# The end of a recurrence rebuilt: head outputs split first, fetches in order of need, spatial weights in their own buffers

## The reference, cut to what matters

```python
a = _rms_norm(h, g_mix[l])
p = a @ w_in[l]
p_sgu, p_rwkv, p_gate = jnp.split(p, [2 * D_A, 2 * D_A + C_B], axis=-1)
y_a = _sgu_branch(p_sgu, ...)      # z = gelu(p_sgu); u, v = split(z); v = layer_norm(v) * w + b
                                   # per chunk of 128 tokens and group of 128 columns:
                                   # s = u * (tril(sgu_w) @ v + sgu_b);  y_a = s @ w_proj_a
y_b = _rwkv7_branch(p_rwkv, ...)   # a recurrence over tokens, 16 heads of 64;  y_b = o @ w_proj_b
mixed = sigmoid(gate_a) * y_a + sigmoid(gate_b) * y_b
h = h + mixed @ w_out[l]           # then a feed-forward net and the last norm
```

## Time and profile before

| | |
|---|---|
| median of 3 runs | 3925.5 us (3919.31 to 3929.22) |
| profiled execution | 3924.53 us; its span 3922.7 us, so 1.8 us lie around the span |
| PE busy | 3692.0 us, 94% of the span |
| DVE, ACT, POOL busy | 1805.7, 1325.9, 295.7 us |
| mean granted clock of PE | 0.976 of full speed |
| chain that ended last | PE 86%, DVE 5%, ACT 5%, issue 2%, DMA 1% |

### The profile page before, as it was taken

The page is one execution under the profiler, slowest core; times in us unless marked ns, Lnnn a source line. Parts: engine busy times, 40 slices in busy tenths (PEclk is TensorE's granted clock), DMA queues, the critical chain, the costliest instruction groups (busy, mean ns, idle before and its releaser), DMA issues.

```text
span 3922.7 us, 53647 instructions
## 1 busy us (share of the span) xinstructions
PE 3692.0 (94%) x23179; PEld 3000.0 (76%) x23179; DVE 1805.7 (46%) x2513; ACT 1325.9 (34%) x2053; POOL 295.7 (8%) x328
## 2 busy tenths in 40 slices
PE   7989999988899998999998999998999999599998
PEld 6777888867678886888886778886877777478887
DVE  4334434444443444543343344344656656445443
ACT  4444322333332232232234443224332333343222
POOL 1001100100010011110010011012000000000001
PEclk9999999989999999999999999998999999799999
DMA  6212323311122332332331123233222212332332
GB/s 208 65 49 70 97 91 102 96 55 52 61 92 91 100 100 75 97 94 90 103 96 54 52 78 97 92 97 98 78 58 62 79 53 67 125 111 89 104 94 69
DMA packets 333231, 337.44 MB, mean 86 GB/s; under 512 B 11857, under 2 KB 323779, under 8 KB 332484
## 3 DMA queue, kind: packets, MB, share of 16 engines
q1 hardware_dynamic: 332578, 333.89, 27.6%
q10 hardware_dynamic: 418, 0.12, 0.0%
HBM read 319.29 MB, written 14.68 MB: 85 GB/s over the span
## 4 chain that ended last, share of the span: by engine, by line
PE 86%; DVE 5%; ACT 5%; issue 2%; DMA 1%; ACTq 0%; POOL 0%; SPq 0%; POOLq 0%; DVEq 0%
PE P L99 85%; ACT sA L114 2%; ACT hi L113 1%; PE P L102 1%; DVE lo L117 1%; DVE x L117 0%; DVE mp L122 0%; DVE ds L125 0%; DVE rw_S L117 0%; DMA scr<-held_dram 0%; ACTq L154 0%; ACT scr L114 0%; DMA vg<-held_v_dram 0%; DVE st L134 0%; DMA rows<-in_shift_b_dram 0%
## 5 line engine op out<-in xcount | busy, mean ns | idle before, releaser
L117 DVE TENSOR_TENSOR lo<-raw,hi 128x1024 fp32r<-128x1024 f32 (+2 forms) x617 | 738.7, 1198 | 1177.6 <-ACT hi L113 1176.9
L99 PE MATMUL P<-aH,lo 128*128 128x512 f32 x2840 | 1142.6, 402 | 28.6 <-DVE q L125 11.4
L99 PE MATMUL P<-aH,hi 128*128 128x512 f32 x2840 | 1114.6, 392 | 0.0
L99 PE MATMUL P<-aL,hi 128*128 128x512 f32 x2840 | 1114.4, 392 | 0.0
L113 ACT ACTIVATE hi<-raw 128x1024 fp32r<-128x1024 f32 (+2 forms) x617 | 610.5, 991 | 1033.3 <-PE P L99 1027.2
L99 PEld LDWEIGHTS P<-aH,lo 128*128 128x128 f32 x2840 | 538.7, 190 | 160.8 <-issue 21.2
L99 PEld LDWEIGHTS P<-aH,hi 128*128 128x128 f32 x2840 | 538.0, 189 | 115.3
L99 PEld LDWEIGHTS P<-aL,hi 128*128 128x128 f32 x2840 | 539.3, 190 | 111.6 <-issue 5.4
L99 PE MATMUL P<-bH,lo 128*128 128x512 f32 x1088 | 426.1, 392 | 16.0 <-DVE bL L117 16.0
L99 PE MATMUL P<-bH,hi 128*128 128x512 f32 x1088 | 424.9, 391 | 0.0
L99 PE MATMUL P<-bL,hi 128*128 128x512 f32 x1088 | 424.9, 391 | 0.0
(11 more groups left out here) (284 smaller groups left out, 3884.5 us busy)
## 6 DMA issues: line engine op xcount, KB each, us to landing
raw<-in_w_ffn_in_dram SPq DMA_DIRECT2D x176, 512.0 KB, 3.5
raw<-in_w_in_dram SPq DMA_DIRECT2D x163, 512.0 KB, 3.8
raw<-in_w_ffn_out_dram SPq DMA_DIRECT2D x96, 384.0 KB, 3.0
raw<-in_w_ffn_dram SPq DMA_DIRECT2D x36, 512.0 KB, 3.6
raw<-in_w_o_dram SPq DMA_DIRECT2D x26, 512.0 KB, 3.5
raw<-in_w_ffn_dram SPq DMA_DIRECT2D x32, 384.0 KB, 3.1
raw<-in_w_mem_kv_dram SPq DMA_DIRECT2D x16, 512.0 KB, 4.3
raw<-in_w_ffn_out_dram SPq DMA_DIRECT2D x16, 512.0 KB, 3.4
```

Of the source, the lines that this page charges most:

```text
L99: return self.e.matmul(out, l, r, start=start, stop=stop, skip_group_check=skip) if self.e else Nothing()
L117: return self.e.tensor_tensor(out, a, b, op) if self.e else Nothing()
```

## The change

- `rw_store` of all eight pairs stands ahead of everything else behind the recurrence. On ACT the eight `bH` splits now come before the gelu of v.
- The last 12 triples of the held products are told to need the end of pair 6, so they go behind the recurrence and no longer between its last steps.
- SP's fetches have a new order: v in four pieces, each with its own semaphore; the spatial weights, the two norm vectors and the bias; the first two tiles of u; the first four gates; then `x`, which came first.
- `wsn` no longer lies in a buffer of the recurrence, nor does `hold1`; `wsn` has a semaphore of its own.
- The layer norm took three DVE operations of 1024 columns a tile (subtract and scale, times weight, plus bias). It now takes two of each half (`scalar_tensor_tensor` of 128x512), first all first halves, then all second halves; groups 0 to 3 of `sgu_mix` need only the first. The inverse deviation is made by one Ln and one Exp over all four tiles.
- The planner's numbers for `side` changed, and with them where its steps fall among the triples.

The diff, cut to its core:

```diff
-    side = [Step("load_v", needs=[("end", 6)], lat=1.0)]
-    side += [Step("rw_store", p, lat=0.8, needs=[("end", p)], gives=[("o", 6)] if p == 6 else []) for p in range(7)]
-    side += [Step("sgu_stats", q, lat=3.0) for q in range(4)]
-    side += [Step("rw_store", 7, lat=0.8, needs=[("end", 7)], gives=[("o", 7)]), Step("sgu_load")]
-    side += [Step("load_gate", i) for i in range(4)] + [Step("load_u", g, needs=[("held",)]) for g in range(2)]
-    side += [Step("sgu_turn", pe=0.9, lat=2.0)] + [Step("sgu_norm", q, lat=2.5) for q in range(4)]
+    side = [Step("load_v", needs=[("end", 6)])]
+    side += [Step("rw_store", p, far=0.0, dve=0.62, wait=0.7, hold=p == 7, needs=[("end", p)], gives=[("o", p)]) for p in range(8)]
+    side += [Step("sgu_load"), Step("first_u", needs=[("held",)]), Step("load_gates"), Step("load_x_back")]
+    side += [Step("sgu_gelu", q, lat=3.0 if q == 0 else 1.0) for q in range(4)] + [Step("first_gates")]
+    side += [Step("sgu_stats", q, dve=1.5, hold=True) for q in range(4)] + [Step("sgu_inverse", lat=7.0), Step("sgu_turn", pe=0.9, dve=1.4, hold=True)]
+    side += [Step("sgu_norm", q, 0, dve=1.55, hold=True) for q in range(4)]
+    side += [Step("sgu_norm", q, 1, far=0.0, dve=1.55, gives=[("ln", q)]) for q in range(4)]
     for g in range(8):
-        side += [Step("sgu_mix", g, pe=1.8, lat=1.0, far=3.5, gives=[("sgu", g)])]
+        side += [Step("sgu_mix", g, pe=1.8, needs=[("ln", 3)] if g >= 4 else [], lat=1.0, far=3.5, dve=1.3, gives=[("sgu", g)])]
...
+    held = jobs_steps(held_jobs(), 1)
+    for s in held[len(held) - 12:]:
+        s.needs += (("end", 6),)
...
-        e.dma(m["vg"][:, :, :], d["held_v"]).then_inc(*S.v_in.up(0, by=16))
+        for q in range(4):
+            e.dma(m["vg"][:, q, :], d["held_v"][:, q, :]).then_inc(*S.v_in[q].up(0, by=16))
...
+        e.stt(y, y, ag[:, 0:1], m["lnw"][:, n], ALU.subtract, ALU.mult).then_inc(*S.evict.up())
+        e.wait_ge(*S.act_turn.at("ln"))
         e.wait_ge(*S.evict.now())
+        e.stt(y, y, rs, m["lnb"][:, n], ALU.mult, ALU.add).then_inc(*S.evict.up(("ln", q, j)))
...
-    at("wsn", [8, 128], off=big + 16384 + 12288)
-    at("wsT", [8, 128], off=ex)
+    at("wsn", [8, 128], off=ex)
+    at("wsT", [8, 128], off=ex + 4096)
...
-    at("hold1", [S_], off=regions[-1][0])
+    at("hold1", [S_], off=ex + 8192)
```

More of the change, by code:

```diff
@@ L450, in the_order @@
     pairs = [[s for p in range(u, 8, 2) for s in pair_steps(p, u)] for u in range(2)]
[L451 to L456 removed]
+    side = [Step("load_v", needs=[("end", 6)])]
[5 more added lines that the diff above has]
+    side += [Step("sgu_norm", q, 1, far=0.0, dve=1.55, gives=[("ln", q)]) for q in range(4)]
     for g in range(8):
[L458 removed]
+        side += [Step("sgu_mix", g, pe=1.8, needs=[("ln", 3)] if g >= 4 else [], lat=1.0, far=3.5, dve=1.3, gives=[("sgu", g)])]
     proj_b = mix_jobs("b", "w_proj_b_2", "rw", [("o", 6)], [("o", 7)])
     proj_a = mix_jobs("a", "w_proj_a_2", "sgu", [("sgu", 6)], [("sgu", 7)])
[L461 removed]
+    held = jobs_steps(held_jobs(), 1)
+    for s in held[len(held) - 12:]:
+        s.needs += (("end", 6),)
+    main = held + abreast(proj_b[:2]) + jobs_steps(proj_b[2:]) + abreast(proj_a[:2]) + jobs_steps(proj_a[2:])
     stage([6, 7], *pairs, side, main, even=2)
@@ L523, in __init__ @@
         self.kv_out, self.kv_in = [t(f"kv_out{l}") for l in range(DEPTH)], t("kv_in")
-        self.x_spill, self.x_back, self.sgu_in, self.out = t("x_spill"), t("x_back"), t("sgu_in"), t("out")
+        self.x_spill, self.x_back, self.sgu_w_in, self.sgu_in = t("x_spill"), t("x_back"), t("sgu_w_in"), t("sgu_in")
+        self.out = t("out")
         self.held_out = [t(f"held_out{i}") for i in range(2)]
         self.held_in, self.gate_in = [t(f"held_in{i}") for i in range(2)], [t(f"gate_in{i}") for i in range(4)]
-        self.v_in = t("v_in")
+        self.v_in = [t(f"v_in{q}") for q in range(4)]
         self.lora_in = [t(f"lora_in{u}") for u in range(2)]
@@ L1041, in sgu_turn @@
     def sgu_turn():
-        e.wait_ge(*S.sgu_in.at(0))
+        e.wait_ge(*S.sgu_w_in.at(0))
         for b in range(2):
@@ L1051, in sgu_mix @@
         b = 4 + g % 2
-        e.wait_ge(*S.evict.at(("ln", 3)))
+        e.wait_ge(*S.evict.at(("ln", 3, g // 4)))
         e.wait_ge(*S.evict.at(("ws", 1)))
@@ L1458, in rw_store, with sgu_gelu @@
         e.act(m["bH"][:, p, :], m["o"][:, p, :], ACT.Copy).then_inc(*S.act_turn.up(("rw", p)))
[L1460 to L1463, removed]
+    def sgu_gelu(q):
+        e.wait_ge(*S.v_in[q].at(0))
+        e.act(m["vg"][:, q, :], m["vg"][:, q, :], ACT.Gelu).then_inc(*S.act_turn.up(("vg", q)))
     def load_u(g):
@@ L1477, in sgu_mix, with first_gates, sgu_inverse @@
             load_u(g + 1)
[L1479 to L1482, removed]
+    def first_gates():
+        load_u(0)
+        load_u(1)
+        for i in range(4):
+            load_gate(i)
+    def sgu_inverse():
+        a = st[:, 8:24].rearrange("p (q n) -> p q n", n=4)
+        e.wait_ge(*S.evict.at(("aggr", 3)))
+        e.act(a[:, :, 2], a[:, :, 1], ACT.Ln, 1.0, eps(1)).then_inc(*S.act_turn.up())
         e.wait_ge(*S.act_turn.now())
-        e.act(rs, rs, ACT.Exp, -0.5).then_inc(*S.act_turn.up(("ln", q)))
+        e.act(a[:, :, 2], a[:, :, 2], ACT.Exp, -0.5).then_inc(*S.act_turn.up("ln"))
     def finish():
@@ L1496, in scalar_program @@
                 rw_level_a=rw_level_a, rw_init=rw_init, rw_start=rw_start, rw_step_b=rw_step_b, rw_out=rw_out, rw_var=rw_var,
-                rw_store=rw_store, load_v=load_v, load_u=load_u, load_gate=load_gate,
-                sgu_stats=sgu_stats, sgu_mix=sgu_mix, finish=finish, split=split, evict=evict)
+                rw_store=rw_store, sgu_gelu=sgu_gelu, first_gates=first_gates,
+                sgu_inverse=sgu_inverse, sgu_mix=sgu_mix, finish=finish, split=split, evict=evict)
     for name, *args in K.order:
@@ L1938, in sgu_stats @@
     def sgu_stats(q):
-        y, bs, ag, rs = m["vg"][:, q, :], m["bs"][:, q, :], st[:, 8 + 4 * q:10 + 4 * q], st[:, 10 + 4 * q:11 + 4 * q]
+        y, bs, ag = m["vg"][:, q, :], m["bs"][:, q, :], st[:, 8 + 4 * q:10 + 4 * q]
         e.wait_ge(*S.act_turn.at(("vg", q)))
@@ L1945, in sgu_stats, with sgu_norm @@
         e.aggr(ag, bs).then_inc(*S.evict.up(("aggr", q)))
[L1946 to L1950, removed]
+    def sgu_norm(q, j):
+        n = slice(512 * j, 512 * j + 512)
+        y, ag, rs = m["vg"][:, q, n], st[:, 8 + 4 * q:10 + 4 * q], st[:, 10 + 4 * q:11 + 4 * q]
         e.wait_ge(*S.sgu_in.at(0))
-        e.wait_ge(*S.evict.at(("centred", q)))
-        e.tt(y, y, m["lnw"][:, :], ALU.mult).then_inc(*S.evict.up())
+        e.stt(y, y, ag[:, 0:1], m["lnw"][:, n], ALU.subtract, ALU.mult).then_inc(*S.evict.up())
+        e.wait_ge(*S.act_turn.at("ln"))
         e.wait_ge(*S.evict.now())
-        e.tt(y, y, m["lnb"][:, :], ALU.add).then_inc(*S.evict.up(("ln", q)))
+        e.stt(y, y, rs, m["lnb"][:, n], ALU.mult, ALU.add).then_inc(*S.evict.up(("ln", q, j)))
     def sgu_mix(g):
@@ L2174, in sgu_load, with first_u, load_gates, load_x_back @@
         e.dma(m["sb"][0:1, :], d["sgu_b_2"].rearrange("a g i -> a (g i)")).then_inc(*S.sgu_in.up(0, by=16))
[L2176 to L2180, removed]
+    def first_u():
+        load_u(0)
+        load_u(1)
+    def load_gates():
+        for i in range(4):
+            load_gate(i)
+    def load_x_back():
+        for k in range(KT):
+            e.wait_ge(*S.operand_lo.at(("rw", "s", k)))
+        e.dma(m["x"][:, :, :], d["spill"].rearrange("p (k n) -> p k n", n=S_)).then_inc(*S.x_back.up(0, by=16))
     def finish():
@@ L2189, in sync_program @@
     todo = dict(load_mem=load_mem, mem_store=mem_store, mem_first=mem_first, mem_values=mem_values, first_end=first_end,
-                rw_begin=rw_begin, evict=evict, load_v=load_v, load_u=load_u, load_gate=load_gate, sgu_load=sgu_load,
-                sgu_mix=sgu_mix, rw_store=rw_store, finish=finish, split=split)
+                rw_begin=rw_begin, evict=evict, load_v=load_v, first_u=first_u, load_gates=load_gates, sgu_load=sgu_load,
+                sgu_mix=sgu_mix, load_x_back=load_x_back, finish=finish, split=split)
     for name, *args in K.order:
```

6 lines of the change are left out of this document (3 added, 3 removed).

## The result

The changed kernel takes 3888.65 us (median of 4 runs, 3884.29 to 3890.42), the kernel before 3924.82 beside it; the ratio is 0.9907 (95% interval 0.989 to 0.9924). The forecast was 3886, with a range of 3875 to 3902. So the medians differ by 36.2 us. The profiled execution took 3890.36 us with a span of 3888.6; the spans of the two profiles differ by 34.1 where 38.3 were forecast.

What follows compares the result with a forecast made beforehand. PE, busy 94% of the span, bounds the kernel, so gains come only from its waits and low clock. Savings of 6.4, 3.4, 4.2 and 24.3 us make 38.3: 3924.5 - 38.3 = 3886.2, range 3875 to 3902.

Steps and rivals of the forecast that it cites:

- (a): Last chunks of the recurrence: moving held triples out brings the mean matmul 6.4 us earlier, 3.2 if DVE bounds.
- (b): From mean matmul to last output `o`: without triples and an eviction ahead, 12.5 us instead of 15.9, gaining 3.4.
- (c): From `o` to `proj_b`, the wait for `bL`: ACT splits heads first, 6.7 us instead of 10.9, gaining 4.2.
- (d): `proj_b` with the weight turn: 43.6 + 1.0 + 1.9 us, without waits if gates arrive, some 3 us of margin.
- (e): Mixes: two at 3.9 us, a 3.7 us wait, 3.2 for half clock, six at 11.8; `proj_a` starts at 3427.7.
- from `proj_a` on: The rest of the span, same dense PE work in both kernels: as long as before, 456.7 us.
- rival B: Fetches still late, so PE stalls in `proj_b` 3 to 10 us plus 2 of clock: 3892 to 3898; 12 in 100.
- Rival D: Clock falls in the chunks or up to `proj_b` and stays low through it: 3950, slower by 24; 2 in 100.

Runs made afterwards that it cites:

- e6: Changed kernel with the twelve held triples put back among the last chunks and around the variance; 3897.44 us, 0.993 of the kernel before.
- e1: Changed kernel with three extra 128x512 matmuls behind each of the eight mixes; 3888.76 us, 0.9919 of the kernel before.
- e4: Changed kernel with the gelus of v again ahead of the bH splits on ACT, v still in four pieces; 3899.05 us, 0.9945 of the kernel before.
- e5: Changed kernel with the mix bias added by a 128-row identity matmul in place of a single-row one; 3875.93 us, 0.987 of the kernel before.
- e8: Changed kernel with the gelus of v ahead of the bH splits and v fetched in one piece; 3900.42 us, 0.9939 of the kernel before.
- e9: Changed kernel with the old norm of three 1024-column DVE operations a tile, all needed by every mix; 3893.14 us, 0.9932 of the kernel before.
- e11: Changed kernel with norm steps placed earlier and the bias over 128 rows, mixes still one after another; 3873.62 us, 0.9889 of the kernel before.
- e7: Changed kernel with SP's group of fetches back in its old place and order, x first; 3904.39 us, 0.9946 of the kernel before.
- e2: Changed kernel with statistics and norm halves placed earlier, removing PE's wait before the third mix; 3888.2 us, 0.9914 of the kernel before.
- e3: Changed kernel with the norm placed earlier and the mixes spread among triples of proj_b and proj_a; 3872.44 us, 0.9879 of the kernel before.

## Why the prediction was right, and where it was not

| step | forecast | measured in the profile |
|---|---|---|
| (a) mean matmul | 3339.4 (6.4 earlier) | 3336.48: 7.3 earlier of its own, 2.0 from ahead |
| (b) mean to the last `o` | 12.5 | 12.45 |
| (c) `o` to `proj_b` | 6.7 | 6.6 |
| (d) `proj_b` with the turn | 46.5 | 46.2 |
| (e) two mixes and the wait | 7.6 | 7.55 |
| (e) six mixes | 15.0 | 23.0 |
| from `proj_a` on | 456.7 | 456.4 |

**(a)** was a little small: the stretch from the held eviction to the mean took 27.6 us where it had been 34.9. The last chunks of the changed kernel on DVE, for the earlier trace rows:

```profile
3326.40 0.28 DVE L125 SCALAR_TENSOR_TENSOR rw_St<-P,rw_dc,rw_SD 128x64 f32<-128x64 f32 x1 [0.15 <-PE P L99]
...
3328.18 0.28 DVE L125 SCALAR_TENSOR_TENSOR rw_St<-P,rw_dc,rw_SD 128x64 f32<-128x64 f32 x1 [0.16 <-PE P L99]
```

A chunk without a triple takes 1.78, with one 2.68, so a triple cost 0.90, where half a triple had given 0.35 and I doubled it. Why it cost more than its own 0.68 on PE is open. I had the direction of the risk wrong: I feared that DVE would keep half.

**(b), (c)** have the right sum, and e6 shows that its parts are not separate gains. That (b) came out to 0.05 us is luck. The second matmul of this stretch ran at half clock in the changed kernel's profile and at full clock in those of e1, e4, e5, e8, e9 and e11, which have the same work here and took 11.0 us. The changed kernel, then e9_norm3:

```profile
3339.30 2.07 PE L99 MATMUL P<-rw_r,c 128*128 128x512 f32 x2 [1.72 <-ACT rw_r L113]
```

```profile
3338.98 1.12 PE L99 MATMUL P<-rw_r,c 128*128 128x512 f32 x2 [1.72 <-ACT rw_r L113]
```

**(c)'s** reason, the order on ACT, is right: put back, it costs 7.8 or 11.9 us by whether v comes in pieces. My sentence that the pieces cost nothing holds; that they are worth 4 us shows only in the old order. The rule for transfers of 1 MiB, which I took from the Trainium skill ("DMA: Bandwidth & Descriptors", "Measured (HBM→SBUF…)"), is not borne out as a reason against them here: the first quarter is there in 4.0 us, the whole in 8.2.

**(d)** held with no wait, and rival B stayed away: ACT had the first gate at 3372.95, inside my 3370 to 3374. e7 shows what rival B costs when it comes: 12.7 us of wait, where I had 3 to 10.

**(e)** is the step that failed, by 8.0 us: the half clock of the six mixes, put at 3.2 us, cost 11.2. The sentence was "It restarts at half clock ... and I take 3.2". A spell at half clock behind the wait was right (e5 has one too). That the mixes would end it was wrong: I let them regain the clock as in the window behind the old norm wait, and that window (0.93) held mixes between triples. e2 shows that mixes alone lose the clock without any wait, e3 that triples between them keep it, e5 that the bias over 128 rows does. The question could have been asked beforehand: the kernel before never ran one mix directly behind another, and the change's order showed that it would.

That the total came within 3 us of the forecast is in part luck. The 8.0 us lost at the mixes stood against 0.9 more in (a), 2.0 of difference between executions and 0.8 of small terms: 38.3 - 8.0 + 3.7 = 34.0. Without the 2.0, the tails give 32.0 of the 38.3. Rival D did not come; all of `proj_b` ran at 0.96.

## What to carry to other kernels

An order of work can take something away that nobody wrote down: triples between odd matmuls filled no wait, but they kept PE's clock up, so ask of each block that a change makes contiguous how its matmuls run by themselves. Look for stretches in which PE is busy at a granted clock of 0.5; they show in no list of waits. When two parts of a change cover the same wait, undo them one by one and both together, or each will be priced wrongly. And move filler out of a latency-bound loop only until the clock falls.

## What the runs showed of the hardware

- PE at 1.2 GHz while never idle: 22.9 us of fp32 mixes with single-row matmuls, clock 0.52; with 128 rows in their place 0.99, back within 5 us of the restart behind a wait. The Trainium skill ("TensorE: Matmul & The Clock Gate", "Loop structure matters more than you think") puts a cold PE down to long waits between matmuls. The trace of e2_early had no wait and still fell from full clock to 0.50, so here a wait was not needed.
- The 128-row bias with the identity made a mix shorter at full clock as well, 1.75 against 2.1 from one to the next (3401.74 to 3403.88 in the changed kernel), though it has the same columns. Why is open.
- Executions of the same matmuls reached one place anywhere from 3299.99 to 3318.07 us, and the four runs of e2_early span 3874.05 to 3897.55. Stretches cut out of the profiles at one common instruction tell a few us where the medians of four runs can't, but each is one execution: a stretch with the same work took 44.2 to 46.7 us, by its granted clock.
